# Twelve tiles of projection A per modulation block instead of six, with the modulation summed in columns and part sums kept outside PSUM

## The reference, cut to what matters

```python
mod = c_act @ ada_w[l] + ada_b[l]            # 2048 -> 6144: shift, scale, gate
shift, scale, gate = ...                     # 2048 each
h = rms_norm(x, pre_gain[l]) * (1.0 + scale) + shift
proj = h @ w_in[l]
pa = proj[..., :COLS_A]                      # r, k, v (1024 each) and two LoRA inputs of 64
z_a = proj[..., OFF_ZA:OFF_B]                # 1024
```

## Time and profile before

| | us |
|---|---|
| median of three runs | 2263.45 |
| profiled execution | 2264.23 |
| its span | 2262.6 |
| TensorE busy | 2213.1 |
| VectorE busy | 1534.3 |
| ScalarE busy | 1106.0 |
| DMA queue of the stream, share of 16 engines | 50.5% |

### The profile page before, as it was taken

How to read it: one execution, slowest core, us unless ns; L and a number is a source line. 1 busy time by engine, 2 the same in 40 slices (tenths; PEclk the granted TensorE clock), 3 DMA queues, 4 the chain that set the end, 5 groups by cost and what they waited for, 6 DMA issues and landing times.

```text
span 2262.6 us, 40660 instructions
## 1 busy us (share of the span) xinstructions
PE 2213.1 (98%) x15228; PEld 1871.0 (83%) x15228; DVE 1534.3 (68%) x2326; ACT 1106.0 (49%) x1741; POOL 124.5 (6%) x128
## 2 busy tenths in 40 slices
PE   7999999999999999999999999999999999999998
PEld 3688887788888888888888887888888888888887
DVE  6768776767766567678666666665566566566766
ACT  2344454555544456465455555544444444445454
POOL 0011000000000010120000002000000000000203
PEclk9999999999999999999999999999999999999999
DMA  9989643333333466665633435555555555555552
GB/s 390 378 327 344 243 142 126 126 130 133 121 124 132 152 225 217 220 205 178 206 128 133 140 126 192 181 180 188 183 190 183 190 179 194 181 190 182 181 185 85
DMA packets 116079, 424.86 MB, mean 188 GB/s; under 512 B 13200, under 2 KB 13456, under 8 KB 115696
## 3 DMA queue, kind: packets, MB, share of 16 engines
q1 hardware_dynamic: 107136, 390.68, 50.5%
q0 software_dynamic: 8816, 32.38, 4.1%
HBM read 414.62 MB, written 8.39 MB: 187 GB/s over the span
## 4 chain that ended last, share of the span: by engine, by line
PE 90%; DVE 4%; ACT 2%; DMA 2%; issue 1%; SPq 0%; DVEq 0%; ACTq 0%
PE ps L2091 48%; PE ps L2092 23%; PE ps L2209 5%; PE ps L2471 3%; DMA raw<-in_stream 1%; PE ps L2472 1%; PE ps L2622 1%; ACT whi L700 1%; DVE wlo L1261 1%; PE ps L2131 1%; PE ps L2144 1%; PE ps L2145 0%; PE ps L2146 0%; DMA xt<-in_x 0%; DVE acc L1292 0%
## 5 line engine op out<-in xcount | busy, mean ns | idle before, releaser
L2091 PE MATMUL ps<-acts,whi 128*128 128x512 f32 x3456 | 1255.0, 405 | 6.3 <-DVE stage L1267 4.9
L1261 DVE TENSOR_TENSOR wlo<-raw,whi 128x1024 fp32r<-128x1024 f32 x647 | 805.3, 1253 | 602.3 <-ACT whi L700 599.9
L700 ACT ACTIVATE whi<-raw 128x1024 fp32r<-128x1024 f32 x671 | 703.9, 1058 | 713.9 <-PE ps L2092 633.2
L2092 PE MATMUL ps<-acts,wlo 128*128 128x256 f32 x3456 | 968.2, 280 | 0.0
L2091 PEld LDWEIGHTS ps<-acts,whi 128*128 128x128 f32 x3456 | 649.3, 188 | 175.2 <-issue 12.9
L2092 PEld LDWEIGHTS ps<-acts,wlo 128*128 128x128 f32 x3456 | 653.2, 189 | 4.5 <-issue 3.3
L2091 PE MATMUL ps<-hidn,whi 128*128 128x512 f32 x1280 | 452.6, 398 | 2.1 <-DVE s L1267 1.8
L2092 PE MATMUL ps<-hidn,wlo 128*128 128x256 f32 x1280 | 357.4, 279 | 0.0
L2091 PEld LDWEIGHTS ps<-hidn,whi 128*128 128x128 f32 x1280 | 240.1, 188 | 64.6 <-DVE s L1267 4.1
L2092 PEld LDWEIGHTS ps<-hidn,wlo 128*128 128x128 f32 x1280 | 241.3, 188 | 0.5 <-issue 0.5
L700 ACT ACTIVATE half<-ps 128x256 f32<-128x256 f32 (+1 forms) x341 | 129.3, 386 | 76.6 <-PE ps L2092 50.3
(11 more groups left out here) (340 smaller groups left out, 2023.7 us busy)
## 6 DMA issues: line engine op xcount, KB each, us to landing
raw<-in_stream SPq DMA_DIRECT2D x735, 512.0 KB, 3.9
graw<-in_ada_gate POOLq DMA_DIRECT2D x32, 512.0 KB, 5.9
gate_dram<-stage POOLq DMA_DIRECT2D x32, 128.0 KB, 2.6
gab<-gate_dram POOLq DMA_DIRECT2D x8, 512.0 KB, 5.0
xt<-in_x SPq DMA_DIRECT2D x1, 2048.0 KB, 9.2
xt<-in_x POOLq DMA_DIRECT2D x1, 2048.0 KB, 8.6
ple_dram<-pr__111 POOLq DMA_DIRECT2D x4, 512.0 KB, 3.6
pj<-ple_dram POOLq DMA_DIRECT2D x1, 2048.0 KB, 12.4
```

Source lines behind the costliest of these rows:

```text
L700: return nc.scalar.activation(dst, src, ACT.Copy)
L1261: tt(wlo[:, n % SPLIT, :], raw[:, g % RAW, :], whi[:, n % SPLIT, :].bitcast(F32), ALU.subtract).then_inc(raw_used, 1)
L2091: mm(ps[bank + n][:, :], whi[:, n0 % SPLIT, c:c + P], act[:, off + kt + k, :], start=kt + k == 0, stop=False)
L2092: ins = mm(ps[bank + n][:, 0:T], wlo[:, n0 % SPLIT, c:c + P], act[:, off + kt + k, 0:T], start=False, stop=kt + k == last)
```

## The change

`WITH_ADA` becomes 15 A, 1 P and 12 W. The opening then holds 42 W tiles; the rest holds 22. `UNITS` lists the opened tiles in pairs (output block, quarter of the channels, pair of banks). A pair of banks passes from one output block to another, so a sum can end before its output block is complete: ScalarE copies it to `rkvz` (`part_out`), and what `use` adds later for the other channels is first summed into `wt` and then added. The twelve products with zeros go, since the first product of a sum now starts it. A P tile becomes 8 products, each with 128 columns of the tile as weights and the one column `cact` as moving data; the sum over `acc` has the same form; so the copy by ScalarE and the turning go. The scaled channel tiles are handed over two at a time. In the rest VectorE takes two gate tiles beside a weight tile instead of one.

```diff
-WITH_ADA = "AAAAPAWPAWAPWAPWAAWAAW"
+WITH_ADA = "AAAA" + 6 * "AW" + "PAW" + 2 * "AAW" + "WWW"
+UNITS = ((0, 0, 0), (1, 0, 1), (2, 0, 2), (3, 0, 0), (4, 0, 1), (5, 0, 2),
+         (3, 1, 0), (4, 1, 1), (5, 1, 2), (6, 0, 0), (6, 1, 0), (7, 0, 1),
+         (7, 1, 1), (5, 2, 2), (6, 2, 0), (7, 2, 1), (0, 1, 2), (0, 2, 2),
+         (6, 3, 0), (7, 3, 1), (0, 3, 2))
+OPENED = 2 * len(UNITS)
+REST = ((1, 2), (2, 2), (3, 4), (4, 4), (5, 6))
+PREVIOUS = [max((v for v in range(u) if UNITS[v][2] == UNITS[u][2]), default=None) for u in range(len(UNITS))]
+STARTS = [u for u, v in enumerate(PREVIOUS) if v is None or UNITS[v][0] != UNITS[u][0]]
+ENDS = [u for u in range(len(UNITS)) if u not in PREVIOUS or PREVIOUS.index(u) in STARTS]
...
+            def part_out(w):
+                u = (w - SPLIT) // 2
+                if w % 2 == 0 or u not in ENDS[:-1]:
+                    return
+                blk_, _, at = UNITS[u]
+                act.wait_ge(quarters, used(WA0 + 2 * u + 1))
+                for n in range(2):
+                    p = blk_ % 2 * 4 + 2 * n
+                    copy(rkvz[:, p:p + 2, wa_at[blk_]:wa_at[blk_] + T], ps[2 * at + n][:, :].rearrange("p (a t) -> p a t", a=2)
+                         ).then_inc(s.part_out, 1)
             for b in range(4):
-                act.wait_ge(s.row_ps, b + 1)
-                for n in range(2):
-                    copy(half[0:1, 2 * n:2 * n + 2, :], ps[6 + n][0:1, :].rearrange("p (a t) -> p a t", a=2)).then_inc(s.row_out, 1)
                 act.wait_ge(s.mod_done, b + 1)
+                for c in range(4 * b, 4 * b + 4, 2):
+                    for x in (c, c + 1):
+                        nc.scalar.activation(scr0[:, x, :], scr0[:, x, :], ACT.Identity, bias=mod[:, x:x + 1], scale=gpre[:, x:x + 1]
+                                             ).then_inc(s.h_done, 1)
+                    act.wait_ge(s.h_done, c + 2)
+                    copy(acts[:, c:c + 2, 0:T], scr0[:, c:c + 2, :]).then_inc(s.acts_hi, 2)
...
-                    if n == 3 and b < 3:
+                    if n == 2 and b < 3:
                         modulation(b)
-                    if n == 8 and b < 3:
-                        rows_lo(b)
+                    if n in (3, 4) and b < 3:
+                        rows_lo(b, n - 3)
...
+            for r, (blk_, first) in enumerate(REST):
+                for j in range(first, 8):
+                    split(WA0 + w + AHEAD)
+                    w += 1
+                    for _ in range(2 if j < 7 and m < 2 * KT else 0):
                         dst = gacc[:, m // KT * CW:m // KT * CW + CW]
                         dve.wait_ge(gate_in[m % 4], 16 * (m // 4 + 1))
                         dve.wait_ge(s.gate_used, m + 4)
                         stt(dst, graw[:, m % 4, :], cact[:, m % KT:m % KT + 1], dst, ALU.mult, ALU.add).then_inc(s.gate_used, 1)
                         m += 1
+                if r == 0:
+                    last, _, at = UNITS[-1]
+                    dve.wait_ge(quarters, 4 * (SPLIT + OPENED))
+                    dve.wait_ge(s.part_out, 2 * len(ENDS) - 2)
+                    for n in range(2):
+                        dst = rkvz[:, last % 2 * 4 + 2 * n:last % 2 * 4 + 2 * n + 2, wa_at[last]:wa_at[last] + T]
+                        tt(dst, ps[2 * at + n][:, :].rearrange("p (a t) -> p a t", a=2), dst, ALU.add).then_inc(evac_done, 2 * EARLY)
+                for n in range(4):
+                    first_half(wt[:, n, :], n, 4 * EARLY + 4 * r + n)
+                for n in range(4):
+                    dve.wait_ge(evac_done, 4 * EARLY + 4 * r + n + 1)
+                    dst = rkvz[:, blk_ % 2 * 4 + n, wa_at[blk_]:wa_at[blk_] + T]
+                    V.do(tt(dst, dst, wt[:, n, :], ALU.add))
+                V.wait()
...
-                for n in range(2):
-                    ins = mm(ps[6 + n][0:1, :], cact[:, j:j + 1], raw[:, g % RAW, n * 512:(n + 1) * 512], start=first, stop=False)
+                for n in range(8):
+                    ins = mm(ps[6][:, n:n + 1], raw[:, g % RAW, n * P:(n + 1) * P], cact[:, j:j + 1], start=first and n == 0, stop=False)
...
+                if w % 2 == 0 and u in STARTS and PREVIOUS[u] is not None:
+                    pe.wait_ge(s.part_out, 2 * ENDS.index(PREVIOUS[u]) + 2)
...
-            for n in range(2 * EARLY):
-                mm(ps[n][:, :], ident, half[:, 0:2, :].rearrange("p a t -> p (a t)"), start=True, stop=False)
...
                 for n in range(8):
-                    ins = nc.tensor.transpose(ps[6][:, n:n + 1], half[0:1, n // 2, n % 2 * P:(n % 2 + 1) * P], ident[0:1, 0:1])
+                    ins = mm(ps[6][:, n:n + 1], acc[:, b * CW + n * P:b * CW + (n + 1) * P], ones[:, 0:1], start=False, stop=n == 7)
...
                     if kind == "W":
                         waiting.append((g, m))
-                while len(waiting) > (TAIL if b < 3 else 0):
-                    opened_tile(*waiting.pop(0))
+                        if len(waiting) > TAIL:
+                            opened_tile(*waiting.pop(0))
+            while waiting:
+                opened_tile(*waiting.pop(0))
+            pe.wait_ge(s.part_out, 2 * len(ENDS) - 2)
+            w = OPENED
+            for r, (blk_, first) in enumerate(REST):
+                for j in range(first, 8):
+                    use(WA0 + w, act=acts, kt=2 * (j - first), last=KT - 1 - 2 * first, off=2 * first,
+                        evac=None if r == 0 else (4 * EARLY + 4 * r - 4, 0))
+                    w += 1
```

More of the change, by code:

```diff
@@ L521, in block_of_two_layers @@
             ada_used = sem("ada_used")
[L522 to L523 removed]
+            part_out = sem("part_out")
             gate_ps = sem("gate_ps")
@@ L539, in block_of_two_layers @@
         eye = con[:, C_EYE:C_EYE + CH]
+        wa_at = [(OR, OK, OV, OZ)[blk_ // 2] for blk_ in range(8)]
         def per_chunk(c):
@@ L756, in _ @@
                         copy(whi[:, w % SPLIT, :], raw[:, g % RAW, :]).then_inc(hi_done, 1)
-            def early_out(x):
-                act.wait_ge(quarters, used(WA0 + 6 * EARLY + 2 * x + 1))
-                for n in range(2):
-                    p, at = x % 2 * 4 + 2 * n, (OR, OR, OK)[x]
-                    copy(rkvz[:, p:p + 2, at:at + T], ps[2 * x + n][:, :].rearrange("p (a t) -> p a t", a=2)).then_inc(evac_done, 2)
-            for w in range(8 * EARLY, 8 * EARLY + AHEAD):
-                split(WA0 + w)
[L767 to L773, removed]
+                        part_out(w)
+            for w in range(OPENED, OPENED + AHEAD):
+                split(WA0 + w)
+                part_out(w)
+            w = OPENED
+            for blk_, first in REST:
+                for j in range(first, 8):
+                    split(WA0 + w + AHEAD)
+                    part_out(w + AHEAD)
+                    w += 1
                 for n in range(4):
-                    second_half(n, WA0 + 8 * b + 7)
+                    second_half(n, WA0 + w - 1)
             for j in range(2):
@@ L2160, in _ @@
                 pe.wait_ge(raw_used, taken(max(g for kind, g, j in opening(b - 1) if kind == "A")))
-                for n in range(2):
-                    ins = mm(ps[6 + n][0:1, :], ones[:, 0:1], acc[:, b * CW + n * 512:b * CW + (n + 1) * 512], start=False, stop=True)
-                ins.then_inc(s.row_ps, 1)
-                if waiting:
-                    opened_tile(*waiting.pop(0))
-                pe.wait_ge(s.row_out, 2 * b + 2)
+                if b:
+                    pe.wait_ge(s.mod_done, b)
                 for n in range(8):
-                    ins = nc.tensor.transpose(ps[6][:, n:n + 1], half[0:1, n // 2, n % 2 * P:(n % 2 + 1) * P], ident[0:1, 0:1])
+                    ins = mm(ps[6][:, n:n + 1], acc[:, b * CW + n * P:b * CW + (n + 1) * P], ones[:, 0:1], start=False, stop=n == 7)
                 ins.then_inc(s.mod_ps, 1)
-                if waiting:
-                    opened_tile(*waiting.pop(0))
-                pe.wait_ge(s.mod_done, b + 1)
                 first = True
@@ L2175, in _ @@
                     if kind == "P":
+                        pe.wait_ge(s.mod_done, b + 1)
                         modulated(g, m, first)
                         first = False
[L2178 to L2179 removed]
                     if kind == "W":
                         waiting.append((g, m))
[L2182 to L2187 removed]
+                        if len(waiting) > TAIL:
[3 more added lines that the diff above has]
+            pe.wait_ge(s.part_out, 2 * len(ENDS) - 2)
+            w = OPENED
+            for r, (blk_, first) in enumerate(REST):
+                for j in range(first, 8):
+                    use(WA0 + w, act=acts, kt=2 * (j - first), last=KT - 1 - 2 * first, off=2 * first,
+                        evac=None if r == 0 else (4 * EARLY + 4 * r - 4, 0))
+                    w += 1
+            pe.wait_ge(evac_done, 4 * EARLY)
             for j in range(2):
```

64 lines of the change are left out of this document (23 added, 41 removed).

## The result

The changed kernel takes 2272.71 us (median of 8 runs, 2268.22 to 2275.99), the kernel before 2264.78 in the same comparison (8 runs, 2263.14 to 2267.36): ratio 1.0031, 95% interval 1.0022 to 1.0040. It is slower by 0.3%; forecast was 2262.3, a hair faster than the 2263.45 known then (the kernel before is itself 1.3 us slower with eight runs than with those three). The time lies inside the range (2253 to 2273), at its upper edge, and the likeliest case had the sign wrong.

What follows compares the result with a forecast made beforehand. It took the stream to bound the old opening, then TensorE the new opening and VectorE the rest: 180.8 + 83.8 = 264.6 against 265.8, -1.2 us, so 2263.0 profiled and median 2262.3; range 2253 to 2273.

Steps and rivals of the forecast that it cites:

- likeliest case: Whole kernel: the forecast of 2262.3 us, -1.2 us against before, with 0.41 for 2258 to 2268.
- Start, 41.6: Kernel start: modulation block 0 ready at 41.6 us, not 39.1, as the clock falls to 1.2 GHz in the P tiles.
- Rival 1: Start and rest: clock holds through P tiles, gate tiles land in time, no cold end; 8.2 us below forecast, 2254; chance 0.31.
- the gate's sums: Earlier profile, 271.45 to 274.94 us: 32 one-column products, clock 0.83 from 275 to 285; evidence for the clock falling.
- Opening, S = 180.8: Opening with 42 W tiles: TensorE is the longest, blocks 38.1 us apart, and it ends at 180.8 us.
- VectorE bounds the rest at 3.72 per tile: The 22 tiles after the opening: VectorE needs 3.72 us per tile with two gate tiles, against TensorE's 2.83.
- Landing of the gate tiles, +1.5: Rest: reusing a gate buffer takes 7.5 us against 7.44 available, just at the edge; costs +1.5 us, bounds 0 and 14.
- R: Time of the 22 tiles after the opening: 81.3 + 1.0 + 1.5 = 83.8 us.
- the prediction's own sign of being wrong, 88: Rest: the forecast is wrong if the rest takes over 88 us or under 78.
- Rival 2: Rest: DMA becomes the bound as gate tiles land in 7.6 to 9.3 us; 2269 to 2276; chance 0.25.
- The sum: End of the rest: S + R = 180.8 + 83.8 = 264.6 us against 265.8, so -1.2.

Runs made afterwards that it cites:

- gate_small_dma: Changed kernel, but gate tiles after the first four loaded only in their first 32 columns, VectorE's sums unchanged; ratio to the kernel before 0.9995.
- changed_again: The changed kernel run once more without any edit, to see the spread; ratio to the kernel before 1.0030.
- gate_neither: Changed kernel with gate products of 16 columns and gate tiles behind the first four loaded in 32 columns only; ratio to the kernel before 0.9912.
- gate_narrow_sum: Changed kernel, but each gate product takes 16 columns instead of 1024, gate tiles still loaded whole; ratio to the kernel before 0.9982.
- gate_spread: Changed kernel with five gate tiles moved beside the opening's last tiles, 27 spread over the rest, at most two beside one; ratio to the kernel before 0.9951.
- gate_on_pe: gate_spread with four gate tiles given to TensorE, one at each of the rest's first four block changes; ratio to the kernel before 0.9936.
- first_rows: Changed kernel with only the first five P tiles and first sum in the old row form (512 moving columns); ratio to the kernel before 1.0012.
- rows_on_pe: gate_on_pe with the first five P tiles and the first sum in the old row form; 2251.33 us, ratio to the kernel before 0.9931.
- before_columns: Kernel before with only P tiles and sums over acc in column form, without ScalarE's copy and the turning; ratio to the kernel before 1.0027.

## Why the prediction was wrong, step by step

- **Start, 41.6.** Right for this execution: 40.44. In the others with this opening it was 40.5 to 44.0. The clock fell where it was said to: the five P tiles took 13.54 us (said 14.0), the sum 3.55 (3.5), the squares 8.65 (9.5). Rival 1, whose clock held through these tiles, falls with it. The Trainium skill ("TensorE: Matmul & The Clock Gate", Part 1) has the gate follow how busy TensorE has been. With "busy" as this profile counts it the clock would have held by that; the 16 us with 15.98 busy at 0.60 speak against it, as the gate's sums had the earlier trace rows.
- **Opening, S = 180.8.** Right: 180.07. Chain to the first tile 5.9 (5.7), loss in the cold first tile 2.1 (1.5; the tile took 4.97 us, a later one 2.88), blocks 39.2, 38.1 and 37.0 apart (38.1). `part_out` cost nothing: TensorE has no gap from 60 to 80 or 140 to 160.
- **VectorE bounds the rest at 3.72 per tile.** Right: 3.72. TensorE's pauses were said as 5.5, 5.6, 3.9, 3.9, together 19; measured 7.4, 7.1, 1.9 and 5.3, together 21.7, with VectorE's waits for gate tiles in them, and 15.4 without these (gate_small_dma).
- **Landing of the gate tiles, +1.5. This is the step that failed.** I set the use of a buffer, "just at the edge", 7.5 against 7.44, with the *median* landing of 5.6, and took a value near the lower bound. The median came to 5.9 (6.4 in changed_again), which makes the loop 7.8 against 7.44, over its limit already; and the slowest took 7.5. A loop at its limit pays for each late one and gains nothing from an early one. Of the 7.44 us, 5.5 are left between the start of an issue and the next use; the five tiles that VectorE waited for could be used only 6.5 to 7.3 us after the start of theirs. VectorE waited 6.3 us, 4.8 more than the term (7.2 in changed_again), and with these waits gone in gate_small_dma TensorE stood 6.3 us less and the time from block 3 on was 5.0 shorter. R was 89.7 and not 83.8, past the prediction's own sign of being wrong, 88. The other 1.1 of the 5.9 is a balance of small things: VectorE's first remainder came 1.8 us after 180.07 and not 1.1, it waited 0.5 for a weight copy, the last two tiles took 7.3 and not 6.7, and its other work took some 0.7 less.
- **Rival 2** (slower, by the landing, 2269 to 2276, "it decides from about 5.5 us to landing") named the right place and sign. That the median, 2272.7, lies in the middle of its range is in part luck: its prices were for 7.6 and 9.3 us to land, with 8.4 to 15 us lost, where 5.9 and 6.3 were measured, and the profiled execution took 2268.2. What I held against it, eight stream buffers full at the end of the opening, did not keep VectorE from waiting for gate tiles, which have a queue and four buffers of their own.
- **The sum.** -1.2 us was the difference of two terms of over 20 us, each good to a few. That is no sign at all, and the chances nearly said so; the likeliest case should have been weighed by the one term whose bounds (0 to 14) were wider than the sum. With 6.3 in place of 1.5 the forecast is 2267.1: the sign turns, and 5.6 us to the median are still missing.

The median is 7.9 us over that of before, the profiled execution 4.0. The other 4 or so are not in this profile. What speaks for the opening: seven profiled executions have the changed kernel's opening, and block 0 is ready in them either at 40.4 to 41.3 or at 43.7 to 44.0. Block 3 parts them more sharply. It is ready at 154.7 to 155.2 in three (changed kernel, changed_again, gate_neither), which are 2.6 to 5.6 us faster than the median of their kernel, and at 157.5 to 157.9 in four (gate_small_dma, gate_narrow_sum, gate_spread, gate_on_pe), which are 0.8 to 3.6 slower. gate_narrow_sum had an early block 0 and lost 2.2 us later, between blocks 1 and 2: TensorE waited 0.45 us for a P tile's data at 96.5, and its clock was 0.50 from 99.3 to 102.7. So the usual execution of this opening may well end some 3 us later than the profiled one. It would also explain why first_rows gains 0.2% by its median and next to nothing in its profile. It is not shown, as each run has a trace of one execution only.

## What to carry to other kernels

When work is moved away from beside other work, re-price what is left on every engine and queue that serves it, here VectorE and a loop of four buffers: 18 tiles moved into the opening won 23 us, and the gate's tiles, left with half the cover, took it back. If two bounds come out within a per cent of each other (7.5 and 7.44), expect to pay for the spread of both, and don't read much from an experiment that removes one: remove both. And a lead of some tiles is no cover at a block change when the evacuation stands behind that lead on the same engine; there another engine's pause is room for the very work that causes it.

## What the runs showed of the hardware

- Back-to-back products with one moving column did not keep TensorE's clock up: from 24 to 40 us it was busy 15.98 of 16 us and was granted 0.60, with 0.54 from 26 to 40: most of it at the 1.2 GHz level. It stayed there over the pause behind it until the first tile had run some 4 us. A single P tile or sum between ordinary tiles, 16 such products, mostly left it at 1.00 (it took 1.84 us, as at 57.07 in the changed kernel). In the nine profiled executions whose later P tiles and sums are columns, that held for 52 of 54. The two others are those before which TensorE had stood: 0.45 us for data in gate_narrow_sum (clock 0.50 from 99.3 to 102.7) and 0.86 us in rows_on_pe (0.50 from 59.1 to 62.6). In before_columns it fell at the sum that followed 1.7 us of standing (0.53 from 98 to 104).
- The moment of the change varies between executions with the same instructions on TensorE up to there. The 32 squares, which begin at half pace (3 to 4 in a us, later 6 to 7), took 8.65 us in the changed kernel and 10.04 in gate_on_pe. In the P tiles behind them the clock fell 4.0 us after their start in the one and 2.0 in the other, and block 0 was ready 3.3 us later.
- Landing of a 512 KB gate tile depends on what else is loaded: 5.9 us median and 7.5 at most in the changed kernel, with three transfers wanted per 3.72 us (6.4 and 7.6 in changed_again); 6.5 and 8.9 with VectorE no longer holding the buffers; 7.5 median in gate_spread, where VectorE yet waited only 1.9 us, since it wants a tile less often. What counts is landing against the loop, not landing alone.
